# The first modulation fetched in four pieces of 256 columns, its bias rows read through the ScalarE queue and added on VectorE, and the first weights behind x

## What is computed

```
c_act = silu(c)
mod = c_act @ ada_w[0] + ada_b[0]                    # 1024 x 6144, sh1, sc1, g1, sh2, sc2, g2 of 1024 each
h = rms_norm(x, norm_g[0, 0]) * (1 + sc1) + sh1
z = gelu(h @ a_w_in); u, v = split(z)                # 1024 x 2048
v = layer_norm(v); mixed = einsum(w_s, v) + b_s      # causal mix over chunks of 128 tokens
y = (u * mixed) @ a_w_out
```

## Time and profile before

| what | value |
|---|---|
| median of 3 runs | 1545.44 us (1545.17 to 1547.06) |
| time of the profiled execution | 1545.76 us |
| its span | 1543.5 us |
| TensorE busy | 1503.5 us, 97% |
| VectorE busy | 1068.7 us, 69% |
| ScalarE busy | 689.3 us, 45% |
| GpSimd busy | 275.2 us, 18% |
| chain that ended last | PE 81%, DVE 10%, ACT 2%, DMA 2%, issue 2% |
| moved by DMA | 203.33 MB, 38.5% of 16 engines' span on the main queue |

### The profile page before, as it was taken

The page is one execution under the profiler, slowest core; times in us unless marked ns, Lnnn a source line. Parts: engine busy times, 40 slices in busy tenths (PEclk is TensorE's granted clock), DMA queues, the critical chain, the costliest instruction groups (busy, mean ns, idle before and its releaser), DMA issues.

```text
span 1543.5 us, 20887 instructions
## 1 busy us (share of the span) xinstructions
PE 1503.5 (97%) x8203; PEld 1248.0 (81%) x8203; DVE 1068.7 (69%) x1588; ACT 689.3 (45%) x1200; POOL 275.2 (18%) x206
## 2 busy tenths in 40 slices
PE   4999999999999999989999999999999999999998
PEld 3888888888888897977778988888888888777777
DVE  6798688889989763258885785666634734588574
ACT  3433552322314454357774641323223544677771
POOL 0200013223232000059881011111100011100000
PEclk9999999999999999999999999999999999999999
DMA  9675256578585214330000254434423222112201
GB/s 331 245 259 191 82 192 239 186 249 307 190 274 190 92 51 142 105 115 2 2 1 29 82 208 165 144 120 141 164 82 109 86 87 78 55 60 75 77 8 55
DMA packets 108807, 203.33 MB, mean 132 GB/s; under 512 B 6042, under 2 KB 13479, under 8 KB 108711
## 3 DMA queue, kind: packets, MB, share of 16 engines
q1 hardware_dynamic: 108710, 202.01, 38.5%
HBM read 199.90 MB, written 2.10 MB: 131 GB/s over the span
## 4 chain that ended last, share of the span: by engine, by line
PE 81%; DVE 10%; ACT 2%; DMA 2%; issue 2%; SPq 1%; POOL 1%; DVEq 0%; ACTq 0%
PE PS L2245 46%; PE PS L2198 21%; DVE MACC L1327 3%; PE PS L2580 3%; PE PS L2607 2%; DVE WL L1293 2%; PE PS L2570 2%; PE PS L2510 1%; PE PS L2269 1%; POOL MROW L506 1%; DMA MRAW<-in_ada_w_dram 1%; DMA X<-in_x_dram 1%; DMA RAW<-in_ff_w_out_dram 1%; PE PS L2572 1%; DMA RAW<-in_ff_w_in_dram 1%
## 5 line engine op out<-in xcount | busy, mean ns | idle before, releaser
L730 ACT ACTIVATE WH<-RAW 128x2048 fp32r<-128x2048 f32 (+1 forms) x109 | 204.4, 1887 | 363.9 <-DMA RAW<-in_ff_w_in_dram 223.7
L1293 DVE TENSOR_TENSOR WL<-RAW,WH 128x2048 fp32r<-128x2048 f32 (+1 forms) x105 | 265.3, 2547 | 119.8 <-ACT WH L730 119.7
L506 POOL PARTITION_ALL_REDUCE MROW<-MACC x26 | 123.3, 4744 | 602.2 <-DVE MACC L1327 514.9
L2245 PE MATMUL PS<-WH,HIDh 128*128 128x512 f32 (+1 forms) x576 | 217.4, 377 | 0.0
L2245 PE MATMUL PS<-WH,HIDl 128*128 128x512 f32 (+1 forms) x576 | 217.3, 377 | 0.0
L2245 PE MATMUL PS<-WL,HIDh 128*128 128x512 f32 (+1 forms) x576 | 217.3, 377 | 0.0
L2245 PE MATMUL PS<-HTh,WH 128*128 128x512 f32 (+1 forms) x520 | 202.4, 389 | 0.4 <-DVE WL L1293 0.4
L2245 PE MATMUL PS<-HTl,WH 128*128 128x512 f32 (+1 forms) x520 | 202.4, 389 | 0.0
L2245 PE MATMUL PS<-HTh,WL 128*128 128x512 f32 (+1 forms) x520 | 202.3, 389 | 0.0
L1327 DVE SCALAR_TENSOR_TENSOR MACC<-MRAW,CS,MACC 128x512 f32<-128x512 f32 x168 | 126.3, 752 | 8.6 <-DMA MRAW<-in_ada_w_dram 1.1
L2245 PEld LDWEIGHTS PS<-WL,HIDh 128*128 128x128 f32 x576 | 108.3, 188 | 20.4
(11 more groups left out here) (351 smaller groups left out, 2998.1 us busy)
## 6 DMA issues: line engine op xcount, KB each, us to landing
MRAW<-in_ada_w_dram SPq DMA_DIRECT2D x44, 1024.0 KB, 7.4
RAW<-in_ff_w_in_dram SPq DMA_DIRECT2D x32, 1024.0 KB, 5.4
RAW<-in_ff_w_out_dram SPq DMA_DIRECT2D x32, 1024.0 KB, 5.1
RAW<-in_w_in_dram SPq DMA_DIRECT2D x16, 1024.0 KB, 5.2
MRAW<-in_w_ada_dram SPq DMA_DIRECT2D x12, 1024.0 KB, 8.8
RAW<-in_a_w_in_dram SPq DMA_DIRECT2D x8, 1024.0 KB, 9.9
MRAW<-in_kv_ada_w_dram SPq DMA_DIRECT2D x8, 1024.0 KB, 5.8
RAW<-in_kv_w_dram SPq DMA_DIRECT2D x6, 1024.0 KB, 5.3
```

The lines of the kernel that those rows point to most:

```text
L506: pool.partition_all_reduce(MROW[:], MACC[:], P, RADD).then_inc(m_red, 1)
L730: act.activation(WH[:, wslot(u), 0:width(u)], RAW[:, u % 4, 0:width(u)], ACT.Copy).then_inc(w_hi, 1)
L1293: dve.tensor_tensor(WL[:, u % 4, 0:width(u)], RAW[:, u % 4, 0:width(u)], WH[:, wslot(u), 0:width(u)].bitcast(F32), ALU.subtract).then_inc( ...
L2245: mm = pe.matmul(po, a, b_, start=(k == 0 and i == 0), stop=(k == KT - 1 and i == len(ops) - 1), skip_group_check=len(ops) > 3)
```

## The change

Seven things are changed, all in the head:

1. **Pieces.** Shift and scale are fetched and accumulated in four pieces `i` of 256 columns each (`head_columns` on SP, `head_acc` on VectorE), shift and scale of the same columns together, in two halves of four row blocks. A piece gives the coefficients of two k. Four buffers `PIECE0` to `PIECE3` of 1 MB take the place of `M3a`, `M3b` and the first use of `MRAW`.
2. **Order of the transfers.** The row of c, piece 0, the four tiles of x, the weights of the first pair of k for both chunks (256 rows x 512 columns each), then piece 1, weights of pair 1, and so on. `PR2`, `WSR`, `LNB`, `BS` come behind all of them. The rows of `PR1` and `PR0` (9 transfers) are issued by ScalarE.
3. **Activations.** ScalarE writes `HIDh` from PSUM itself, and `RB` by a second pass over the same tile; VectorE makes only `HIDl` (`remainder`). `XR` is gone.
4. **Order on TensorE.** `depth(c_, k)` goes pair by pair through both chunks: k = 0, 1 of chunk 0, k = 0, 1 of chunk 1 (three banks), then the next pair. Within a k the four banks are the inner loop. Bank 3 takes the columns, the turned x of k = 2 to 7, the turned `WSR` and the bias in turn; chunk 1's fourth bank is made whole at the end.
5. **Three plain matmuls** of the identity behind each turned tile of x (L2437 of the changed kernel).
6. **The root's table** is loaded ahead of x by a dummy activation.
7. **`MIXC + BS`** moves from GpSimd to VectorE, between `mod_acc` of modulation 4 and `lo(4)`, behind waits for both copies of `MIXC` and for `BS`. The gate rows of modulation 5 are issued behind the second half of chunk 2's weights instead of ahead of it.

```diff
-    XR = at("XR", [P, 4, T], F32, o_y)
-    M3 = [at("M3a", [P, 4, 512], F32, o_w + 24576), at("M3b", [P, 4, 512], F32, o_y + 8192)]
+    PIECE = [at(f"PIECE{i}", [P, KT, 256], F32, (o_mraw, o_mraw + 8192, o_y, o_y + 8192)[i]) for i in range(4)]
...
+        def head_columns(i):
+
+            for h in range(2):
+                ks = slice(4 * h, 4 * h + 4)
+                if i >= 2:
+                    sp.wait_ge(h_acc, 16 * i - 24 + 8 * h)
+                for j in range(2):
+                    src = cols_of(ada[0], D * (1 - j) + 256 * i, 256)[:, ks, :]
+                    p = 2 * (i % 2) + j
+                    sp.dma_start(PIECE[p][:, ks, :], src).then_inc(h_in[i % 2][h], 16)
...
+        sp.dma_start(PR1[C_C:C_C + KT, :], c[0].rearrange("(r p) -> r p", p=P)).then_inc(c_in, 16)
+        head_columns(0)
+        for tt in range(TT):
+            load_x(tt)
+        for c_ in range(2):
+            first_weight(c_, 0)
+        for pair in range(1, 4):
+            head_columns(pair)
+            first_weight(0, pair)
+            first_weight(1, pair)
...
-        first_mod(0)
-        for tt in range(TT):
-            load_x(tt)
-        half_weight(a_w_in[0], D, 0)
         sp.dma_start(WSR[:], a_w_s[0].rearrange("g t s -> t g s")).then_inc(ws_in, 16)
-        first_mod(1, 12)
-        half_weight(a_w_in[0], D, 1)
-        half_weight(a_w_in[0], D + 512, 3)
-        n.chunk = 2
+        n.mod, n.chunk = 4, 2
...
-        for i in range(2, 6):
+        weight(a_w_in[0], 0, between=lambda: mod(0, 5))
+        gate_rows(5, mod_src[0][1], 5, a_mods(1)[0][2])
...
-        pool.wait_ge(mix_e, 2)
-        pool.wait_ge(bs_in, 16)
-        flat = lambda v: v.rearrange("p g t -> p (g t)")
-        pool.tensor_tensor(flat(MIXC[:]), flat(MIXC[:]), flat(BS[:]), ALU.add).then_inc(mix_cr, 1)
...
+        def scaled(k):
+
+            src = PS[:, HEAD_BANK[k], :]
+            act.wait_ge(full, 4 + k + 1)
+            act.activation(HIDh[:, k, :], src, ACT.Identity, scale=AB[:, 0, k:k + 1], bias=AB[:, 1, k:k + 1]
+                           ).then_inc(tile_hi, 1)
             if k >= 2:
                 act.wait_ge(tile_rdy, k - 1)
-            act.activation(RB[:, k % 2, :], src, ACT.Identity, scale=AB[:, 0, k:k + 1],
-                           bias=AB[:, 1, k:k + 1]).then_inc(done, 1)
+            act.activation(RB[:, k % 2, :], src, ACT.Identity, scale=AB[:, 0, k:k + 1], bias=AB[:, 1, k:k + 1]
+                           ).then_inc(x_ev, 1)
...
+            first_hi(0, 0)
+            for pair in range(4):
+                act.wait_ge(coef0, pair + 1)
+                scaled(2 * pair)
+                scaled(2 * pair + 1)
+                first_hi(1, pair)
+                if pair < 3:
+                    first_hi(0, pair + 1)
...
+        rows(PR1, C_NG, norm_g.rearrange("l j (r p) -> (l j r) p", p=P), par1_in)
+        rows(PR0, B_L[0], ada_b.rearrange("l (r p) -> (l r) p", p=P), par0_in)
         act.wait_ge(cols, 1)
         act.activation(CS[:], C1[:, C_C:C_C + 8], ACT.Silu).then_inc(act_c, 1)
...
+        act.wait_ge(pool_c, 2)
+        act.activation(SM[:, 47:48], EPST[:], ACT.Sqrt)
...
+            def head_acc(i, half):
+
+                acc = (MACC, MROW)[i % 2]
+                for k in range(4 * half, 4 * half + 4):
+                    for j in range(2):
+                        a, p = acc[:, 256 * j:256 * j + 256], 2 * (i % 2) + j
+                        src = PIECE[p][:, k, :]
+                        if k == 4 * half and j == 0:
+                            dve.wait_ge(h_in[i % 2][half], 32 * (i // 2 + 1))
+                        if k == 0:
+                            if j == 0 and i >= 2:
+                                dve.wait_ge(m_red, i - 1)
+                            dve.tensor_scalar(a, src, CS[:, 0:1], None, ALU.mult).then_inc(h_acc, 1)
+                        else:
+                            dve.wait_ge(h_acc, 16 * i + 2 * k - 1 + j)
+                            dve.scalar_tensor_tensor(out=a, in0=src, scalar=CS[:, k:k + 1], in1=a,
+                                                     op0=ALU.mult, op1=ALU.add).then_inc(h_acc, 1)
...
+            def head_coefs(i):
+
+                dst = MCOL[:, 0:16].rearrange("p (a c) -> p a c", a=2)[:, :, 2 * i:2 * i + 2]
                 dve.wait_ge(m_red, i + 1)
-                dve.tensor_copy(MCOL[:, 4 * ch:4 * ch + 4], src).then_inc(m_post, 1)
+                dve.tensor_copy(dst, PS[:, 3, 0:4].rearrange("p (a c) -> p a c", a=2)).then_inc(m_post, 1)
                 dve.sem_inc(m_c, 1)
                 n.mod += 1
+                dve.wait_ge(m_post, i + 1)
+                coefs(0, AB, 8, 0, C_NG, slice(2 * i, 2 * i + 2)).then_inc(coef0, 1)
...
+                dve.wait_ge(x_ev, k + 1)
+                dve.tensor_tensor(HIDl[:, k, :], RB[:, k % 2, :], HIDh[:, k, :].bitcast(F32), ALU.subtract
+                                  ).then_inc(tile_rdy, 1)
...
+            head_acc(0, 0)
+            head_acc(0, 1)
+            normed(0)
             dve.wait_ge(full, 4)
-            dve.tensor_copy(C02[:], PS[:, 5, 0:P + PAR2]).then_inc(ev_d, 1)
-            dve.wait_ge(ev_d, 1)
...
-            coefs(0, AB, 8, 0, C_NG, slice(0, 4)).then_inc(coef0, 1)
+            head_coefs(0)
             normed(2)
             normed(3)
             jobs[0] += TT
-            lo_half(0, 0).then_inc(w_first, 1)
-            for k in range(4):
-                if k == 2:
-                    lo_half(0, 1)
-                dve.wait_ge(ev_a, k + 1)
...
+            first_lo(0, 0)
+            remainder(0)
+            head_acc(1, 0)
+            remainder(1)
+            first_lo(1, 0)
+            head_acc(1, 1)
+            first_lo(0, 1)
+            head_coefs(1)
+            for pair in range(1, 4):
+                if pair < 3:
+                    head_acc(pair + 1, 0)
+                remainder(2 * pair)
+                remainder(2 * pair + 1)
+                first_lo(1, pair)
+                if pair < 3:
+                    head_acc(pair + 1, 1)
+                    first_lo(0, pair + 1)
+                    if pair == 2:
+                        dve.wait_ge(m_red, 4)
+                        dve.tensor_copy(C02[:, P:P + PAR2], PS[:, 3, P:P + PAR2]).then_inc(cols, 1)
+                    head_coefs(pair + 1)
             n.group = 3
...
             mod_acc(a_mods[i][0][0])
+            if i == 0:
+                dve.wait_ge(mix_e, 2)
+                dve.wait_ge(bs_in, 16)
+                flat = lambda v: v.rearrange("p g t -> p (g t)")
+                dve.tensor_tensor(flat(MIXC[:]), flat(MIXC[:]), flat(BS[:]), ALU.add).then_inc(mix_cr, 1)
             lo(4 + i)
```

On TensorE (`pe_program`), new:

```diff
+        def head_columns(i):
+
+            pe.wait_ge(h_acc, 16 * i + 16)
+            if i:
+                pe.wait_ge(x_ev, 2 * i)
+            if i == 3:
+                pe.wait_ge(par2_in, 16 * 8)
+                pe.transpose(PS[:, 3, P:P + PAR2], PR2[:], IDENT[0:PAR2, 0:PAR2])
+            acc = (MACC, MROW)[i % 2]
+            for j in range(4):
+                o = 256 * (1 - j // 2) + P * (j % 2)
+                mm = pe.matmul(PS[:, 3, j:j + 1], acc[:, o:o + P], ONES[:], start=True, stop=True)
             mm.then_inc(m_red, 1)
 
-        def turn_x(tt, half):
...
-        column(0, MACC)
-        pe.wait_ge(m_post, 1)
-        column(1, MROW)
-        for tt in range(TT):
-            turn_x(tt, 0)
+            for _ in range(3):
+                pe.matmul(PS[:, 2, 0:P], IDENT[:], IDENT[:], start=True, stop=True)
...
+        def depth(c_, k, after=(None, None, None)):
+
+            pair, u, o = k // 2, 2 * c_ + k // 4, 512 * (k % 4)
+            pe.wait_ge((wp_lo, w_lo)[pair % 2], 2 * (pair // 2) + c_ + 1)
+            h, l = WH[:, u, o:o + 512], WL[:, u, o:o + 512]
+            for i in range(3):
+                if c_ == 0 and i != 1:
+                    pe.wait_ge((tile_hi, None, tile_rdy)[i], k + 1)
+                for b in range(4 - c_):
+                    a = (HIDl if i == 2 else HIDh)[:, k, P * b:P * b + P]
+                    mm = pe.matmul(bank(3 + c_, b), a, l if i == 1 else h, start=(k == 0 and i == 0),
+                                   stop=(k == KT - 1 and i == 2), skip_group_check=True)
+                    if i == 2 and k == KT - 1:
+                        mm.then_inc(full, 1)
+                    elif i == 2 and b == 3 and k == 3:
+                        mm.then_inc(w_used, 1)
+                if after[i] is not None:
+                    after[i]()
+
...
+        for pair in range(4):
+            k = 2 * pair
+            if pair == 0:
+                depth(0, 0)
+            else:
+                depth(0, k, (lambda: turn_later(k + 1), None, None))
+            if pair < 3:
+                depth(0, k + 1)
+                depth(1, k)
+                head_columns(pair + 1)
+                depth(1, k + 1, (lambda: turn_later(k + 2), None, None))
+            else:
+                depth(0, k + 1, (None, lambda: weights_turned(0), None))
```

(8 more changed lines are left out.)

301 lines of the change are left out of this document (117 added, 184 removed).

## The result

The changed kernel takes 1547.75 us (median of 20 runs, 1547.23 to 1550.60), the kernel before 1545.14 (20 runs, 1543.73 to 1547.06). The ratio is 1.0018, with a 95% interval of 1.0012 to 1.0024. The profiled execution took 1547.23 us, with a span of 1545.5 where the one before had 1543.5. It is the fastest of its 20, while the profiled execution before, at 1545.76, is above its median, so the two profiles lie closer together than the medians. Outside the span the launches of the new head take 1.7 to 1.8 us and those of the kernel before 1.9 to 2.4; why was not looked at.

A forecast was written before the change was run, and what follows sets the result against it. TensorE, busy 97% of the span, was taken as the bound, with VectorE's list behind the head releasing mix(0). T0 72.1 + 33.4 = 105.5 against 105.9 gave -0.4 us: 1545.4; 8 in 10 between 1541 and 1550.

The forecast's parts named there:

- The clock falls in the wait: Rival: after TensorE's 5.3 us wait before mix(0) it works at half speed, losing 2.6 us; 1548.0, chance 0.17.
- The start: Head's loads, roots and first tiles: first large matmul at 21.8, 9.5 us earlier than 31.33.
- A piece on VectorE: Head's half-width sums: multiply-add 0.485 us, 0.405 apart when alternating; 6.2 a piece, 24.8 for four against 24.2 before.
- Slower, by the pieces: Rival: head operations on VectorE take 0.58 us, or 1 KB transfers run slow; +3.4 us, 1549.2, chance 0.18.
- One pair: Head, coefficients of one pair of k to the next: 11.9 us, first pair 12.7, pair 3 starting at 58.3.
- T0: End of the copy of MIXC at the head's end, which VectorE's MIXC + BS waits for: 72.1.
- Cold matmuls: Head's first large matmuls run at full speed thanks to the plain matmuls; if not, 1.5 to 2.4 us lost.
- Behind the head: VectorE's list from T0 to mod_acc(6): 33.4 us with a 5.2 us all-reduce, ending at 105.5, 1.6 later than before.
- The gain comes through in part: Rival: T0 3.2 us earlier, short all-reduce up to 2.0 more, mix(0) at 100.5 to 102.3; 1541.5, chance 0.24.
- the likeliest case: The forecast itself: mix(0) starts at 105.5 instead of 105.89, -0.4 us; chance 0.41, range 1543 to 1548.
- The bound: Whole-kernel time: about 0.2%, 3.1 us, is what a measurement can tell from no change.

The follow-up runs named there:

- list_first: Changed kernel with ScalarE's hi(4) ahead of the two MIXC copies and VectorE's lo(4) ahead of the MIXC addition; 1547.07 us, ratio 1.0012.
- stats_first: Changed kernel with VectorE's layer norm of V ahead of the two gate operations that wait for the second all-reduce; 1543.96 us, ratio 0.9988 to the kernel before.
- busy24: Changed kernel with 24 plain identity matmuls on TensorE between chunk 2 and mod_column(6); 1545.93 us, ratio 1.0003 to the kernel before.
- busy48: Changed kernel with 48 plain identity matmuls on TensorE between chunk 2 and mod_column(6); 1549.79 us, ratio 1.0030 to the kernel before.
- no_plain: Changed kernel without the three plain matmuls behind each row tile's transposes in the head; 1549.15 us, ratio 1.0024 to the kernel before.
- busy16: Changed kernel with 16 plain identity matmuls on TensorE between chunk 2 and mod_column(6); 1547.57 us, ratio 1.0016 to the kernel before.
- before_short: Kernel before, with 7 filling tensor_scalar operations on VectorE ahead of mod_acc(6), 3.65 us of them; 1547.75 us, ratio 1.0019.
- filled: Changed kernel with the list_first and stats_first orders, the modulation 6 column copy between two weight remainders, and 7 identity matmuls ahead of mod_column(6); 1540.32 us, ratio 0.9967.

## Why the prediction was right and where it failed

The measured 1547.75 lies in the range, but the forecast was 1545.4, a gain of 0.4 us or none, and the kernel is slower by 0.18%. The rival "The clock falls in the wait", 1548.0, is what happened.

**The start.** Forecast: x tile 0 landed at 12.2, last root 18.4, last V 19.8, first matmul 21.8. Measured: 11.6, 17.8, 19.8, 21.28. Right within 0.6. Five stretches between 6 and 40 us that have the pieces' 1 KB runs in them moved 348 to 380 GB/s; 360 was taken.

**A piece on VectorE.** Fourteen multiply-adds of 128x256 take 5.73 us from 7.89 on, which with the last at 0.48 makes the assumed pitch of 0.405 (one takes 0.475 to 0.486; 0.485 was assumed). The rival "Slower, by the pieces" falls with it.

**One pair.** Forecast 11.9 apart. The coefficients of pairs 1, 2 and 3 were ready at 32.1, 43.9 and 56.2: 11.8 and 12.3. T0 was forecast at 72.1 and came at 71.6; chunk 2 at 77.2.

**Cold matmuls.** Full speed from the first, as chosen. The run without the plain matmuls shows that they are why, and that the choice was worth little: the turns in which the engines wait for each other in a pair hide most of the slow start.

**Behind the head.** Forecast: mod_acc(6) ends at T0 + 33.4 = 105.5, with an all-reduce of 5.2. Measured: 71.6 + 33.4 = 105.0, and 5.19. This term carries the case, and it was right: the head ends 7 us earlier (chunk 2 at 77.2 instead of 84.13), VectorE's list 1.1 later. list_first and stats_first show the two places where it hangs. The rival "The gain comes through in part" asked for a short all-reduce or an earlier T0, and had neither.

**The step that failed** is the end of it, "TensorE is through with chunk 2 at 100.2 and waits 5.3 us. mix(0) starts at 105.5 instead of 105.89", and then nothing: the sum took columns and mix at their old length. Two things were left out of the likeliest case.

First, the clock. The wait was 6.01 us, the clock fell, and busy24 prices the fall at 1.8 us (the rival had 2.6). The argument against it, "nothing in this trace shows a fall once the clock was up", is not true of the trace that it names. In the kernel before, TensorE waits 2.16 us for a weight remainder late in the span, and one microsecond after its return it runs at 0.50 for some 3.4 us:

```profile
1353.00:1357.00 4.00, 1.84 (x10) 1.38 (x10) 3.96 (x4) 3.97 (x5) 0.00 (x0) 1.00 1.02 386
1358.00:1361.00 3.00, 3.00 (x8) 2.32 (x8) 2.77 (x2) 2.97 (x5) 0.00 (x0) 0.50 0.01 3
```

```profile
1356.79 0.47 PE L2198 MATMUL PS<-WH,HTh 128*128 128x512 f32 x1 [2.16 <-DVE WL L1293]
```

There the matmuls stand 0.43 apart instead of 0.23. The page's clock row reads 9 in all 40 slices, because a slice is 38.6 us long; only narrow windows show the fall. So in the trace at hand the clock had already fallen behind a wait less than half as long as the forecast one, and the rival's chance of 0.17 was set without that row. The rule that the prediction cites from the Trainium skill (TensorE: Matmul & The Clock Gate, "What's actually happening") agrees with the waits of 4.9 to 6.0 us: the array that stood idle came back at the lower level.

Second, the copy of the columns, which no case had. VectorE's list is 1.1 us later than before, and the fourth block of the mix asks for a copy at its end. In the kernel before, that copy ended at 108.40, about 1 us ahead of its use (105.89 + 0.79 + three quarters of 3.68 is 109.44). In busy24 the block waits 0.64 us for it, and the wait of 0.55 ahead of the columns is not in that.

Together they turn -0.74 into +2.2: start -0.74, fall +1.8, the copy and what the columns took longer at full speed (5.63 against 4.47) +1.16. The sum on the rows of the rival, +2.2, agrees with the trace only because an overpriced fall made up for the copy. The -0.74 is luck too: this execution had the earliest head of ten. In four other profiles with VectorE's list in the same order (busy48, no_plain, busy24, busy16) mod_acc(6) ended at 105.66 to 106.42, about where the kernel before asked for it, so the forecast start of 105.5 was good and the usual execution gained next to nothing by it.

**The bound.** The prediction took 3.1 us as what a measurement can tell. With 20 runs on each side the interval was 0.12% wide, and the difference of the medians, 2.6 us, was told from none.

**What stays open.** Waits of 4.9 and 6.0 us in front of the columns cost the clock in every profile that had one (four with the new head, one with the old). Shorter waits did not decide it. At this place 1.7 to 2.8 us cost it in four profiles with the new head, and 1.84 us in before_short did not. The wait of 2.16 us near 1357 is a fairer test, as it is in all fourteen profiles, 2.15 to 2.19 us long, with the same work around it: the clock fell behind it in five (the kernel before, the changed kernel, busy24, no_plain, filled) and stayed at 1.00 in nine. So one and the same short wait goes either way by execution, with either head, and before_short's one profile does not show that the old head is safe. What makes the difference was not found out.
